# Reading back half of an expert layer's rows before its last blocks are done, and holding two weight loads behind the first gathers

## The reference, cut to what matters

```
for l in range(2):
    ...                                      # projections, selected attention, gating
    h  = x + merged @ w_out
    xf = rms_norm(h, norm2)                  # 640 x 1024
    group = argmax(xf @ w_rg + b_rg)         # one of 4 groups
    e1, e2 = top2(softmax(logits in that group))           # 2 of its 8 experts
    for e in (e1, e2):                       # 32 experts, hidden width 128
        y_e = (silu(xf @ w_eg[e]) * (xf @ w_eu[e])) @ w_ed[e]
    x = h + weight(e1) * y_e1 + weight(e2) * y_e2
y = rms_norm(x, final_norm)
```

## Time and profile before

| | |
|---|---|
| median of 3 runs | 1464.19 us |
| profiled execution | 1469.72 us |
| its span, first to last instruction | 1468.0 us |
| PE busy | 1323.0 us (90%) |
| DVE busy | 541.5 us (37%) |
| POOL busy | 219.7 us (15%) |
| mean granted TensorE clock | 0.952 |
| DMA, mean over the span | 140 GB/s |

### The profile page before, as it was taken

How to read it: one execution, slowest core, us unless ns; L and a number is a source line. 1 busy time by engine, 2 the same in 40 slices (tenths; PEclk the granted TensorE clock), 3 DMA queues, 4 the chain that set the end, 5 groups by cost and what they waited for, 6 DMA issues and landing times.

```text
span 1468.0 us, 15494 instructions
## 1 busy us (share of the span) xinstructions
PE 1323.0 (90%) x5756; PEld 733.9 (50%) x5756; DVE 541.5 (37%) x1542; ACT 342.6 (23%) x773; POOL 219.7 (15%) x304
## 2 busy tenths in 40 slices
PE   7999898999999996998599989899999999979790
PEld 5654345544444555655385544464444445556450
DVE  1278885100111236321244779831011103452115
ACT  2232466200000100222213325651000010112121
POOL 5011033000000001223240200600000000013313
PEclk9999999999999997999799999999999999979895
DMA  8302102502403316799571110042060060279966
GB/s 237 115 13 59 58 1 70 172 0 70 145 0 121 152 43 227 300 407 392 206 203 58 50 47 34 8 131 104 0 215 0 0 258 29 86 279 410 405 261 237
DMA packets 95485, 205.63 MB, mean 140 GB/s; under 512 B 26465, under 2 KB 35905, under 8 KB 95409
## 3 DMA queue, kind: packets, MB, share of 16 engines
q1 hardware_dynamic: 80800, 178.13, 34.3%
q0 software_dynamic: 14608, 26.49, 5.1%
HBM read 196.29 MB, written 27.78 MB: 153 GB/s over the span
## 4 chain that ended last, share of the span: by engine, by line
PE 81%; DVE 5%; issue 4%; ACT 4%; DMA 3%; PEld 2%; PEldq 1%; POOL 0%; SPq 0%; POOLq 0%; ACTq 0%; DVEq 0%
PE bank L747 34%; PE bank L1029 9%; PE bank L1080 9%; PE bank L1126 8%; PE bank L1137 4%; PE bank L780 3%; PE bank L1113 2%; DMA uv<-xd,mb 2%; PE bank L829 1%; DVE stat L1687 1%; PE bank L1046 1%; PE bank L733 1%; PE bank L933 1%; PE bank L833 1%; DVE x L1821 1%
## 5 line engine op out<-in xcount | busy, mean ns | idle before, releaser
L747 PE MATMUL bank<-ring,xt 128*128 128x512 f32 (+1 forms) x1120 | 434.6, 545 | 7.5 <-DMA ring<-in_w_in 4.5
L747 PEld LDWEIGHTS bank<-ring,xt 128*128 128x128 f32 x1120 | 214.6, 194 | 209.5 <-issue 189.8
L1756 DVE TENSOR_TENSOR scr<-scr,bank 128x512 f32<-128x512 f32 x20 | 13.8, 688 | 368.8 <-PE bank L1029 368.8
L1080 PE MATMUL bank<-ring,xt 128*128 128x512 f32 x320 | 141.3, 594 | 0.0
L541 POOL TENSOR_SCALAR stat<-stat 128x1 f32<-128x1 f32 (+1 forms) x27 | 10.3, 381 | 805.8 <-ACT uv L1213 617.0
L1357 ACT ACTIVATE scr<-bank,stat 128x512 f32<-128x512 f32 x40 | 25.3, 684 | 348.0 <-PE bank L747 348.0
L1080 PEld LDWEIGHTS bank<-ring,xt 128*128 128x128 f32 x320 | 59.3, 190 | 67.0 <-issue 67.0
L780 PE MATMUL bank<-ring,xt 128*128 128x512 f32 x160 | 75.9, 608 | 0.0
L1029 PE MATMUL bank<-ring,att 128*128 128x512 f32 x160 | 72.5, 596 | 2.2 <-ACT sgt L1349 1.8
L1029 PE MATMUL bank<-ring,sgt 128*128 128x512 f32 x160 | 71.9, 592 | 0.0
L747 PE MATMUL bank<-more,xt 128*128 128x512 f32 x160 | 70.3, 592 | 0.0
(11 more groups left out here) (285 smaller groups left out, 1848.7 us busy)
## 6 DMA issues: line engine op xcount, KB each, us to landing
ring<-in_w_in SPq DMA_DIRECT2D x12, 2048.0 KB, 9.2
ring<-in_w_ed SPq DMA_DIRECT2D x32, 512.0 KB, 16.7
ring<-in_w_eg SPq DMA_DIRECT2D x26, 512.0 KB, 10.8
ring<-in_w_eu SPq DMA_DIRECT2D x26, 512.0 KB, 16.8
ring<-in_w_out SPq DMA_DIRECT2D x4, 2048.0 KB, 12.5
more<-in_w_ed SPq DMA_DIRECT2D x14, 512.0 KB, 9.7
qkv<-in_w_eg SPq DMA_DIRECT2D x12, 512.0 KB, 6.3
qkv<-in_w_eu SPq DMA_DIRECT2D x12, 512.0 KB, 7.7
```

The source lines that it names most:

```text
L747: mm = pe.matmul(out, xt[:, k, t * P:(t + 1) * P], rhs[:, k, :], start=(k == 0), stop=(k == KD - 1))
L1080: mm = pe.matmul(banks[5 + n % 3][:, :], xt[:, k, t * P:(t + 1) * P], w[:, k, :], start=(k == 0), stop=(k == KD - 1))
```

## The change

Two things are changed. First, SP makes the load that stands at number 7 only when gather 1 of the layer has landed (`x_in[1]`), and number 9 behind it. Second, the experts are renumbered: the last of each group gets a number from 28 to 31 (`EXPERT_OF`). The two experts of a row are of one group, so the lower number is always below 28, and its k = 1 result is written by the end of block 14. SP now waits for the scatters of blocks 0 to 14 alone and reads the five k = 1 tiles into the qkv buffer; DVE adds weight times these rows to x for tiles 0 and 1 after `hidden_rows` of block 15, and for tiles 2 to 4 after `hidden_rows` of block 16 (`first_of`). After the last scatter only the five k = 0 tiles are read, and `combine` is one step. So that a read of a row not yet written finds numbers, POOL fills the k = 1 half of `yd` once, in layer 0, from the input rows (2.6 MB, DRAM to DRAM). Some buffers move (`fin_gain`, `REST_AT`), and the load of the next layer's first columns or of the final gain is issued ahead of the overflow test.

```diff
+EXPERT_OF = [e for e in range(EXPERTS) if e % NE < NE - 1] + [e for e in range(EXPERTS) if e % NE == NE - 1]
...
-        fin_gain = qkv_flat[:, 2048:2048 + D]
+        fin_gain = more[:, 3072:3072 + D]
...
-        pairs = [w.rearrange("p (k c) -> p k c", k=2) for w in
-                 (uv_flat[:, 0:2048], uv_flat[:, 2048:4096], sgt_flat[:, 512:2560], more[:, 0:2048], more[:, 2048:4096])]
+        last_rows = [uv_flat[:, D * t:D * t + D] for t in range(PT)] + [more[:, 0:D]]
+        first_rows = [qkv[:, t, 0:D] for t in range(NT)]
...
                 sp.wait_ge(unit_done, prior("unit_done", L) + 16)
-                for e in (6, 7):
-                    expert(e, EXPERTS * L + e)
+                expert(6, EXPERTS * L + EXPERT_OF[6])
+                sp.wait_ge(x_in[1], gathers(1) * L + 16)
+                expert(7, EXPERTS * L + EXPERT_OF[7])
                 sp.wait_ge(r_psum, prior("r_psum", L) + NT)
-                expert(9, EXPERTS * L + 9)
+                expert(9, EXPERTS * L + EXPERT_OF[9])
...
+                by_pair = yd.rearrange("(k t p) c -> k t p c", k=2, t=NT)
+                for z in range(YBUF):
+                    sp.wait_ge(y_out[z], scatters(z) * L + 16 * len(range(z, OVER_AT + 1, YBUF)))
+                for t in range(NT):
+                    sp.dma_start(first_rows[t], by_pair[1, t]).then_inc(combine_in[t][1], 16)
...
                 for z in range(YBUF):
                     sp.wait_ge(y_out[z], scatters(z) * L + scatters(z))
                 for t in range(NT):
-                    for k in range(2):
-                        sp.dma_start(pairs[t][:, k, :], yd.rearrange("(k t p) c -> t k p c", k=2, t=NT)[t, k]
-                                     ).then_inc(combine_in[t][k], 16)
+                    sp.dma_start(last_rows[t], by_pair[0, t]).then_inc(combine_in[t][0], 16)
...
                 pool.dma_start(ids, a["ids"]).then_inc(wr_loaded, 16)
+                if L == 0:
+                    pool.dma_start(yd[ROWS:ROWS + SEQ, :], a["x_prompt"][0]).then_inc(yd_set, 16)
+                    pool.dma_start(yd[ROWS + SEQ:2 * ROWS, :], a["x_sample"].rearrange("b t d -> (b t) d")).then_inc(yd_set, 16)
...
+                pool.wait_ge(yd_set, 32)
                 for b in range(XBUF):
...
+                def first_of(t):
+                    then(V.scalar_tensor_tensor(first_rows[t], first_rows[t], pair_at[:, 2, t, 1:2], x[:, t, :],
+                                                ALU.mult, ALU.add))
+
                 for b in range(NB):
                     hidden_rows(b, b % XBUF, b % 2)
                     if b + 2 < NB:
                         rows_out(b + 2, b % 2)
+                    if b >= NB - 2:
+                        for t in (range(2), range(2, NT))[b - NB + 2]:
+                            dve.wait_ge(combine_in[t][1], 16 * L + 16)
+                            first_of(t)
...
                 def combine(t):
-                    for k in range(2):
-                        dve.wait_ge(combine_in[t][k], 16 * L + 16)
-                        ins = V.scalar_tensor_tensor(x[:, t, :], pairs[t][:, k, :], pair_at[:, 2, t, k:k + 1], x[:, t, :],
-                                                     ALU.mult, ALU.add)
-                        if k == 0:
-                            then(ins)
-                    ins.then_inc(x_new, 1)
+                    dve.wait_ge(combine_in[t][0], 16 * L + 16)
+                    V.scalar_tensor_tensor(x[:, t, :], last_rows[t], pair_at[:, 2, t, 0:1], first_rows[t],
+                                           ALU.mult, ALU.add).then_inc(x_new, 1)
```

More of the change, by code:

```diff
@@ L429, in _ @@
                         sp.wait_ge(rows_sent, prior("rows_sent", L) + 1)
-                        expert(1, EXPERTS * L + 1)
+                        expert(1, EXPERTS * L + EXPERT_OF[1])
                     if u == QU:
@@ L481, in _ @@
                     sp.wait_ge(unit_done, prior("unit_done", L) + done)
-                    expert(e, EXPERTS * L + e)
+                    expert(e, EXPERTS * L + EXPERT_OF[e])
                 sp.wait_ge(mt_done, prior("mt_done", L) + 2 * NT)
-                expert(10, EXPERTS * L + 10)
+                expert(10, EXPERTS * L + EXPERT_OF[10])
                 for t in range(NT - 1):
@@ L487, in _ @@
                 sp.wait_ge(unit_done, prior("unit_done", L) + 15)
-                expert(5, EXPERTS * L + 5)
+                expert(5, EXPERTS * L + EXPERT_OF[5])
                 rows_kept(NT - 1)
@@ L500, in _ @@
                         sp.wait_ge(gu_psum[L], (v - PLACES) // 2 + 1)
[L501 removed]
+                        expert_up(v % PLACES, EXPERTS * L + EXPERT_OF[2 * BLOCK_AT[v // 2] + v % 2], up_in[v % PLACES])
                     for v in units:
                         sp.wait_ge(y_psum[L], (v - PLACES) // 2 + 1)
[L504 removed]
+                        expert_down(v % PLACES, EXPERTS * L + EXPERT_OF[2 * BLOCK_AT[v // 2] + v % 2], down_in[v % PLACES])
+                if L + 1 < DEPTH:
+                    sp.wait_ge(y_psum[L], RING_FREE)
+                    key_columns(L + 1)
+                else:
+                    sp.wait_ge(y_psum[L], RING_FREE)
+                    sp.dma_start(fin_gain, a["final_norm"].partition_broadcast(P)).then_inc(s_gain, 16)
+                by_pair = yd.rearrange("(k t p) c -> k t p c", k=2, t=NT)
[3 more added lines that the diff above has]
+                    sp.dma_start(first_rows[t], by_pair[1, t]).then_inc(combine_in[t][1], 16)
                 sp.wait_ge(experts_known, prior("experts_known", L) + 1)
@@ L510, in _ @@
                             row = sp.value_load(over_expert[:, bass.ds(2 * v + (ALWAYS + h), 1)], min_val=0, max_val=EXPERTS - 1)
-                            expert_up(h, EXPERTS * L + row, over_w[L])
-                            expert_down(h, EXPERTS * L + row, over_w[L])
+                            expert_up(REST_AT[h], EXPERTS * L + row, over_w[L])
+                            expert_down(REST_AT[h], EXPERTS * L + row, over_w[L])
                     sp.wait_ge(y_over, earlier(sp) + (16 * REST + 16))
[L514 to L521, removed]
+                    for t in range(NT):
+                        sp.dma_start(first_rows[t], by_pair[1, t]).then_inc(over_w[L], 16)
                 for z in range(YBUF):
@@ L1200, in _ @@
                         pe.wait_ge(h_done[L], b)
-                        up(places[0:2], 0)
+                        up([places[i] for i in REST_AT], 0)
                         pe.wait_ge(h_done[L], b + 1)
@@ L1206, in _ @@
                         pe.wait_ge(y_ready[L], b)
-                        down(places[0:2], 0)
+                        down([places[i] for i in REST_AT], 0)
         @block.scalar
@@ L1510, in tile_route @@
                                     ALU.add).then_inc(chosen_ready, 1)
-                then(V.tensor_tensor(number[:, t, :], chosen[:, t, :], ids[:, 1:EXPERTS + 1], ALU.mult))
+                then(V.tensor_tensor(number[:, t, :], chosen[:, t, :], ids[:, BR + 2 * NT:], ALU.mult))
                 V.tensor_reduce(number_k[:, t, 0:1], number[:, t, :], AX.X, ALU.max)
@@ L1816, in _ @@
                         hidden_rows(v + NB, 0, 0)
-                def combine(t):
-                    for k in range(2):
-                        dve.wait_ge(combine_in[t][k], 16 * L + 16)
-                        ins = V.scalar_tensor_tensor(x[:, t, :], pairs[t][:, k, :], pair_at[:, 2, t, k:k + 1], x[:, t, :],
-                                                     ALU.mult, ALU.add)
-                        if k == 0:
-                            then(ins)
-                    ins.then_inc(x_new, 1)
+                    dve.wait_ge(over_w[L], 96 * REST + 16 * NT)
+                    for t in range(NT):
+                        ins = V.scalar_tensor_tensor(first_rows[t], first_rows[t], pair_at[:, 2, t, 1:2], x[:, t, :],
+                                                     ALU.mult, ALU.add)
+                    ins.then_inc(xin_ready[L], 1)
+                    dve.wait_ge(xin_ready[L], 2 * (NB + REST) + 1)
+                def combine(t):
+                    dve.wait_ge(combine_in[t][0], 16 * L + 16)
+                    V.scalar_tensor_tensor(x[:, t, :], last_rows[t], pair_at[:, 2, t, 0:1], first_rows[t],
+                                           ALU.mult, ALU.add).then_inc(x_new, 1)
                 def finish(t):
@@ L1867, in _ids @@
     pairs = 1 + np.arange(2 * ROWS).reshape(2, NT, P).transpose(2, 1, 0).reshape(P, 2 * NT)
-    return np.concatenate([np.tile(np.arange(BR), (P, 1)), pairs], axis=1).astype(np.float32)
+    units = 1 + np.argsort(EXPERT_OF)
+    return np.concatenate([np.tile(np.arange(BR), (P, 1)), pairs, np.tile(units, (P, 1))], axis=1).astype(np.float32)
 def kernel(**inputs):
```

8 lines of the change are left out of this document (4 added, 4 removed).

## The result

| | kernel before | changed kernel |
|---|---|---|
| median of the timed runs beside each other | 1463.40 us (6 runs) | 1470.13 us (6 runs, 1464.26 to 1473.67) |
| ratio | 1 | 1.0042, interval 1.0022 to 1.0062 |
| profiled execution | 1469.72 us | 1464.26 us |
| mean granted clock in it | 0.952 | 0.955 |

The change makes the kernel about 6 us slower: beyond the predicted 1462.6 us, beyond the range (1457.0 to 1468.6), and on the side that had a chance of 0.20.

What follows compares the result with a forecast made beforehand. It took gather waits to bound the stage's start, the load stream its middle, and the last scatter, reads and DVE's sum its end. -6.0 + 12.1 - 7.7 = -1.6 gave 1462.6 us, range 1457 to 1468.6.

Steps and rivals of the forecast that it cites:

- I take 3.4 in layer 0 and 2.6 in layer 1: -6.0: Start of the expert stages: first gathers land sooner with 3.1 MB of loads moved behind them; -6.0 us, bounds 0 and -8.2.
- The gathers' price: Start of each expert stage: a gather takes 3.7 us, like a scatter of as many places, instead of 7.71 or 6.69.
- PE's side of my sum: First up product of each expert stage: PE can start it 4.1 us sooner in layer 0, 3.1 in layer 1.
- the loads' side: Early expert stage: experts 11 and 12 queue behind the moved loads and end about 1 us later than a full shift.
- the loads only change places: Slower rival, blocks 2 to 10: later loads are pushed back, gathers' gain is lost; +4.4 us, 1468.6; slower rivals together 0.21.
- its neighbour: Slower rival at stage start: a gather takes over 6 us by itself, so moving loads does nothing; +4.4, within the shared 0.21.
- The wait, +12.1: Before block 16's hidden_rows: DVE waits for early reads, +3.7 and +5.0 us, plus 1.7 per layer for PE's slower clock.
- The clock's share: Last down products: after PE idles some 5 us they run at the 1.2 GHz level, +1.7 us in each layer.
- The tail, -7.7: After the last scatter: fewer DVE steps for the sums, -2.5 us in layer 0 and -5.2 in layer 1.
- At nothing: Parts taken as free: the fill of yd near 254 us, steps of tiles 2 to 4, renumbering and the moved next-layer loads.
- The prediction's last step: Whole kernel: the -1.6 us step from the profiled 1469.7 us was applied to the runs' median 1464.2, giving 1462.6.

Runs made afterwards that it cites:

- the kernel with the read-back alone: Changed kernel without the wait on gather 1, so experts 7 and 9 load as before; 1471.87 us, ratio 1.0051 to the kernel before.
- the better version: Changed kernel with only tiles 0 to 2 read early and their steps behind hidden_rows of block 16; 1456.23 us, 0.9945 to the kernel before.

## Why the prediction was wrong

**The step that failed: "I take 3.4 in layer 0 and 2.6 in layer 1: -6.0".** The runs give -1.8 us (+0.9 to -4.4) for this part alone. Two things were behind it.
- The gathers' price. I took 3.7 us from a scatter of as many places. With experts 7 and 9 put back gather 0 of layer 0 lands after 4.2 to 4.6 us and the first four in a median of 5.0 to 5.2, and PE waits for gather 1, issued 1.49 us later, not for gather 0. The up product came sooner by 2.4 to 2.9 us in layer 0 and 1.5 to 1.9 in layer 1 in the kernels with these loads moved, against 4.1 and 3.1 on PE's side of my sum.
- What is left of it at the end. I let 0.7 and 0.5 us go on the loads' side. At block 15 two thirds of the gain are gone, most of it on PE's own side. Over the profiled kernels, eight with the wait ahead of expert 7 alone and four without, an up product begins by so much sooner after gather 0 with the wait (difference of the means, us):

| up product of block | 0 | 9 | 10 | 13 | 15 | 16 |
|---|---|---|---|---|---|---|
| layer 0 | 2.6 | 2.4 | 2.2 | 2.0 | 0.9 | 1.7 |
| layer 1 | 1.7 | 1.5 | 0.0 | 1.5 | 0.5 | 0.8 |

The fall from 3.5 us in both layers at block 13 to 1.4 at block 15 is block 13's own up product: it takes a mean of 4.74 and 5.16 us with the wait and 3.67 and 4.12 without, 2.1 us more in both layers. The mean granted clock over it is 0.55 to 0.80 in twelve of the 16 stages with the wait and 1.00 in the others; without it 0.66 in one of eight and 1.00 in seven. PE has idled for gather 13 or for weights around it in all of them. Why the clock falls so much more often with the wait is not settled: no run changes that idle alone.

The stream of loads itself did come sooner. Its last load, in layer 0, was issued at 691.54 before and at 685.84 in the changed kernel; the last column is the time to landing, before and then now:

```profile
more<-in_w_ed SPq DMA_DIRECT2D x1, 512.0 KB, 15.3
```

```profile
more<-in_w_ed SPq DMA_DIRECT2D x1, 512.0 KB, 14.3
```

That is 130.3 us after gather 0 before, and 126.5 now. In the means of the same twelve it is 130.3 and 127.1, in layer 1 132.2 and 131.2: 4.2 us in both layers. So the rival "the loads only change places" had the time, 1468.6 us for a measured 1470.1 and 1469.0, but not the mechanism. Its point was a stream that moves by less than 1.5 us, and its place PE's idle at block 10, which is 3.03 and 2.47 us in the changed kernel and was 3.61 and 2.17. I gave it and its neighbour 0.21, because the engines had stood idle for 7 us before. That the idle was filled was seen; that the clock would take a part of the gain at block 13 was not.

**The wait, +12.1: right in kind, about 1 us too small.** By the two kernels that differ in it alone it is 13.2 us from block 15's up product on, 14.8 in the stages and 15.9 in the timings. The clock's share was right (3.70 for 1.96, +1.7 a layer, in the changed kernel). The wait hangs on block 14's scatter, which did not come sooner with the gathers: 128.4 us after gather 0 in layer 0, and 128.8 before. In the profiled execution the parts cancelled in layer 0. I had scatter and read too long by about as much, so hidden_rows of block 16 stands 136.9 us after gather 0, as forecast (716.8 - 576.49 - 3.4). And its time before, 711.45, had PE's wait for block 16's weights ahead of it, which I did not see; in the changed kernel that wait is gone. In layer 1 the second read set DVE's start, and in the kernel with the read-back alone tile 1's rows came 5.66 us after their issue, the next row of its chain after a scatter of 3.0:

```profile
1430.48 3.01 DMA yd<-scr,mb
...
1434.17 5.66 DMA qkv<-yd
```

**The tail, -7.7: right.** 2.4 in layer 0 and 5.8 in layer 1 in the first profile (predicted 2.5 and 5.2), 2.5 and 4.5 in the second. The last finish waits 0.81 us for POOL's root and the one before it 0.44, together 0.45 more than before, not the 1.2 I allowed. What I did not see is that this gain depends on the wait: without it the early reads stretch the last scatter by 2.2 to 4.3 us a layer, which is why the better version reads fewer tiles early.

**At nothing: right as far as shown.** The fill of `yd` runs in idle time of the DMA engines, and PE is as busy as before in that stretch. From 245 to 285 us PE is busy for 36.33 us before and 36.34 in the changed kernel. The stretch in which the fill stands out most, before and then now:

```profile
255.00:260.00 5.00, 3.48 (x60) 2.72 (x55) 0.78 (x3) 4.61 (x9) 0.00 (x0) 1.00 0.00 0
```

```profile
255.00:260.00 5.00, 4.28 (x51) 2.94 (x52) 0.00 (x0) 4.75 (x9) 0.00 (x0) 1.00 0.78 282
```

It was not tried by itself.

**The sum by measured parts:** -1.8 for the loads and +7.5 for the read-back, where the prediction had -6.0 and +4.4; of the miss of about 7 us, 4.2 is the loads' part and 3.1 the read-back's. Of the 3.1, the wait counted from block 15's up product gives 1.1; the rest lies inside the interval of the +7.5 (4.7 to 10.4). The prediction's last step carried the sum from one profiled execution to the median by a constant. That execution is no typical one in its stages either: in ten of the twelve comparisons of the table the stages make the other kernel look better than the timing does, by 1.8 us in the mean of all twelve.

## What to carry to other kernels

A step that only has to be done early belongs behind the last instruction of its engine that others wait for; in front of it, it turns a transfer's landing into a wait of the whole chain, and here that placing alone decided between 4 us faster and 6 us slower. Ask of a gain at a stage's start whether the stage's last block comes sooner, look block by block at where it is lost, the granted clock included, and count a wait from the event that releases it, not from the work before it. And read two profiles by stages cut at the same events: whole spans of single executions differed by 5.5 us in parts that the change hardly touched, with the wrong sign.

## What the runs showed of the hardware

- Four indexed gathers of 128 rows, issued 1.3 to 1.7 us apart, land in 5.1 us in the median when no plain load is in flight at their start (4.4 the first, 5.2 the second), and in 7.2 behind the loads of experts 6, 7 and 9.
- The same up product of 32 matmuls takes 3.67 us where the granted clock is 1.00 and 5.1 to 5.3 us where its mean is 0.69 to 0.71 (block 13).
- An indexed scatter that takes 3.2 us alone takes 5.4 to 7.5 when 2.6 MB of plain reads were issued 3.5 to 6.5 us ahead of it, and 3.2 to 4.3 behind 1.6 MB. The Trainium skill, "DMA: Bandwidth & Descriptors", section "Issuing engines are not separate DMA queues", says that transfers of all issuers run on the same 16 engines and interleave; these rows agree with it for SP's reads and POOL's scatter.
